# Attention of a four-layer transformer stack: heads in pairs, scores on two row tiles and values on two column tiles

## Chip, cores and metric

One core of one Trainium2 chip. The metric is the device time of one launch in microseconds (us); the median of several runs counts. "Engines" are TensorE (PE; PEld is its weight load), VectorE (DVE), ScalarE (ACT), GpSimd (POOL) and the DMA queues, of which SyncE (SP) issues the weights.

## What is computed

512 tokens of width 1024 go through two blocks of two layers each, all in float32. Attention stands in five places:

```python
# block 1, layer 0: 8 heads A (64 wide, three dilated windows, mixed by their log-sum-exp), 8 heads B (96 wide)
s = einsum(q, k) * scale;  o = softmax(s) @ v
# block 1, layer 1: 8 heads C, each the difference of two softmaxes
o = (softmax(s0) - lam * softmax(s1)) @ v          # v is 128 wide
# block 2, both layers: 4 heads each of
o_cmp = masked_softmax(q @ kc) @ vc                # 31 compressed keys
o_slc, o_win = causal softmax attention            # all blocks selected at 512 tokens
o = sigmoid(g0) * o_cmp + sigmoid(g1) * o_slc + sigmoid(g2) * o_win
o_fox = softmax(q @ k + c_q - c_k, causal) @ v     # with a decay
```

A's mixture of three windows equals one softmax in which key j counts as often as it lies in a window (`count`, 0 to 3). Around attention stand projections, feed-forward layers, norms and gates.

## The kernel before

Every activation is held transposed, features on the 128 partitions and the 512 tokens in the columns (`S` = 512, `P` = 128, `ST` = 4 tiles of tokens, `HD` = 64). Weights stream in 375 blocks of 512 KB through a ring of two. POOL splits each into a high and a low float32r part (L2131, L2134), the activations are split likewise by ACT and DVE, and TensorE makes three passes (`passes`, L681 to L683) into a PSUM bank. POOL can begin to split a block only when TensorE is done with the block two before it.

The program is written out by hand for each engine; engines meet by counting semaphores, and each engine's list is strictly in order. The stages are `mixer_a`, heads A, `mixer_b`, heads B, the output projection, norms and feed-forward, `mixer_c`, heads C, and so on; then, twice, `project_second`, `heads_second` and `merge`.

Attention (`attention`, one function for each engine) takes the heads one by one, and for each head its four tiles of 128 queries: such a step is a turn (`TURN_AT`). TensorE writes the scores of a turn into one of banks 0 to 3 (L742), three turns ahead of the rest (`AHEAD`), adds a mask or a decay by further matmuls (L745), and for the current turn transposes the exponentials `prob` (L775) into bank 4 or 5 and does one quarter of the values of the head before (L756). DVE takes the negated row maximum (L1648), ACT the exponentials (L1298) and the copy of the transposed ones into `pt` (L1285); for A, DVE makes that copy and multiplies it by `count` (L1639). The exponentials stay unnormalised: `v_ab`, `v_s`, `v_w` and `v_f` carry 64 columns of ones beside 64 of values, so that a 128-column values matmul gives the sum of each query's exponentials, 64 times over, in the other half of the bank. `divided` inverts those (two 32 x 32 transposes and a reciprocal, L1600 to L1603), multiplies by a gate where there is one, and by the values (L1683 to L1686); these steps are put behind later turns (`pending`, `FINISH_LAG`). The C heads differ: two scores for a turn, both banks exponentiated with row sums (`accum_out`), blended on DVE (`mixed`, L1626 to L1630) and then transposed; values there are 128 wide. The list `pending` also carries other DVE work in A (norms, splits and copies of `mixer_b`'s inputs) and in the second block (a convolution).

In `project_second` the three gates of each head are spread over 64 partitions each by six matmuls (`spread_gate`, L1031) into `gates`, and the compressed attention is done unnormalised as well: scores (L1046), exponentials, transposes (L1053), values and sums (`compressed_values`, L1060 and L1061), and division on DVE (L2023 to L2026).

In most runs of instructions a float32 matmul shows as two instructions in the trace.

## Time and profile before

| | us |
|---|---|
| median of 3 runs | 2795.81 |
| lowest and highest run | 2786.32, 2802.13 |
| span of the profiled execution | 2796.3 |
| TensorE busy | 2640.1 |
| DVE busy | 1359.9 |
| ACT busy | 657.1 |
| POOL busy | 1683.9 |

The profile is one execution. An engine's busy time is the union of its instructions; the chain of waits is followed back from the last instruction to what released each step. A time in a row is counted from the start of the span. Several instructions of the same kind in a row are merged into one line with their count, and the line's duration runs from the first start to the last end. A matmul's end is modelled: of two that follow closely, the second starts before the first ends, so the distance of starts says more than the durations. "Granted clock" is TensorE's, as a share of 2.4 GHz.

### The profile page before, as it was taken

Reading aid. Unit: us, or ns where it says so; the run is one execution under the profiler, and the core shown is the slowest. Engines: PE = TensorE matmul, PEld = TensorE weight load, DVE = VectorE, ACT = ScalarE, POOL = GpSimd, SP = SyncE. Lnnn points to the kernel's source line nnn. Section 1 sums busy time; section 2 is a strip of 40 time slices with the busy share of each in tenths; the row PEclk is TensorE's granted clock in tenths of the full one; section 3 lists DMA queues with packets and bytes.
Section 4 is the critical chain, followed back from the end, with each engine's and each line's share of the span. In section 5 each row is a group of like instructions: output and inputs, shape, how many; then the busy total and the mean of one; then the engine's idle time right before and its main releaser. Section 6 shows DMA issues by size and latency. Waiting matters only on the chain.

```text
span 2796.3 us, 30962 instructions
## 1 busy us (share of the span) xinstructions
PE 2640.1 (94%) x11138; PEld 1962.2 (70%) x11138; DVE 1359.9 (49%) x1615; ACT 657.1 (23%) x1110; POOL 1683.9 (60%) x756
## 2 busy tenths in 40 slices
PE   7998989999989978899999889999999899999998
PEld 6635568888867743678888677747888678478886
DVE  7476653220161888562211645565443545645343
ACT  2223423320021146132210231142010211421101
POOL 6603068887757720568887557605888676048785
PEclk9989999999999999999999999999999999999999
DMA  4201012222212210122222122201222222012222
GB/s 158 83 0 38 1 67 91 98 98 98 94 57 98 83 38 1 60 68 97 98 98 98 63 92 91 76 1 60 98 98 98 75 83 83 8 46 98 98 98 83
DMA packets 57543, 207.59 MB, mean 74 GB/s; under 512 B 6512, under 2 KB 6896, under 8 KB 57200
## 3 DMA queue, kind: packets, MB, share of 16 engines
q1 hardware_dynamic: 55872, 199.87, 21.2%
q10 hardware_dynamic: 1584, 6.49, 0.6%
q8 instruction: 64, 1.05, 0.2%
q14 instruction: 23, 0.19, 0.0%
HBM read 204.23 MB, written 2.10 MB: 74 GB/s over the span
## 4 chain that ended last, share of the span: by engine, by line
PE 84%; DVE 12%; POOL 1%; issue 1%; ACT 1%; DMA 0%; DVEq 0%; POOLq 0%; ACTq 0%
PE bank L681 23%; PE bank L683 22%; PE bank L682 22%; PE bank L742 5%; PE bank L756 4%; PE bank L775 2%; DVE region L1610 2%; PE bank L745 1%; DVE negmax L1648 1%; DVE x L1852 1%; PE bank L805 1%; DVE region L1589 1%; DVE prob L1630 1%; DVE moving_lo L1843 1%; DVE moving_lo L1595 1%
## 5 line engine op out<-in xcount | busy, mean ns | idle before, releaser
L2131 POOL TENSOR_TENSOR w_hi<-ring,unit 128x1024 fp32r<-128x1024 f32 x375 | 727.7, 1941 | 1063.2 <-PE bank L683 1058.1
L2134 POOL TENSOR_TENSOR w_lo<-ring,w_hi 128x1024 fp32r<-128x1024 f32 x375 | 955.6, 2548 | 29.5
L681 PE MATMUL bank<-moving_hi,w_hi 128*128 128x512 f32 x2138 | 853.0, 399 | 55.5 <-DVE moving_lo L1843 19.6
L682 PE MATMUL bank<-moving_lo,w_hi 128*128 128x512 f32 x2138 | 841.4, 394 | 0.0
L683 PE MATMUL bank<-moving_hi,w_lo 128*128 128x512 f32 x2138 | 841.2, 393 | 0.0
L681 PEld LDWEIGHTS bank<-moving_hi,w_hi 128*128 128x128 f32 x2138 | 406.5, 190 | 164.5 <-issue 44.8
L683 PEld LDWEIGHTS bank<-moving_hi,w_lo 128*128 128x128 f32 x2138 | 406.6, 190 | 87.2
L682 PEld LDWEIGHTS bank<-moving_lo,w_hi 128*128 128x128 f32 x2138 | 407.4, 191 | 85.4 <-issue 2.9
L742 PE MATMUL bank<-region 64*128 64x512 f32 (+2 forms) x448 | 198.9, 612 | 10.8 <-ACT region L1464 4.1
L1648 DVE TENSOR_REDUCE negmax<-bank 128x1 f32<-128x512 f32 (+1 forms) x224 | 131.8, 602 | 122.4 <-PE bank L745 84.7
L756 PE MATMUL bank<-region 128*128 128x512 f32 (+3 forms) x384 | 167.1, 525 | 1.7 <-ACT region L1285 0.9
L1298 ACT ACTIVATE prob<-bank,negmax 128x512 f32<-128x512 f32 (+1 forms) x224 | 137.1, 615 | 90.0 <-DVE negmax L1648 90.0
L2082 DVE TENSOR_TENSOR region<-region,bank 128x512 f32<-128x512 f32 x64 | 39.7, 683 | 243.3 <-PE bank L683 243.3
L1825 DVE SCALAR_TENSOR_TENSOR region<-x,bank 128x512 f32<-128x512 f32 x32 | 21.3, 686 | 274.1 <-PE bank L683 274.0
L742 PEld LDWEIGHTS bank<-region 64*128 64x128 f32 (+1 forms) x448 | 64.3, 199 | 110.8 <-issue 80.0
L681 PE MATMUL bank<-hid_hi,w_hi 128*128 (+1 forms) x352 | 137.8, 391 | 0.0
L683 PE MATMUL bank<-hid_hi,w_lo 128*128 (+1 forms) x352 | 137.0, 389 | 0.0
L682 PE MATMUL bank<-hid_lo,w_hi 128*128 (+1 forms) x352 | 136.9, 389 | 0.0
L1551 ACT ACTIVATE region<-bank 128x512 f32<-128x512 f32 x64 | 38.3, 598 | 373.8 <-PE bank L683 373.7
L775 PE MATMUL bank<-tabs,prob 128*128 128x128 f32 x624 | 107.6, 287 | 15.1 <-DVE prob L1630 14.7
L775 PEld LDWEIGHTS bank<-tabs,prob 128*128 128x128 f32 x624 | 74.9, 146 | 66.1 <-DVE prob L1630 41.6
L1865 DVE SCALAR_TENSOR_TENSOR region<-bank,cols,region 128x511 f32<-128x511 f32 x44 | 33.0, 749 | 181.5 <-ACT region L1399 181.5
(236 smaller groups left out, 3146.9 us busy)
## 6 DMA issues: line engine op xcount, KB each, us to landing
ring<-in_weights SPq DMA_DIRECT2D x375, 512.0 KB, 3.2
x<-in_x_t ACTq DMA_DIRECT2D x4, 512.0 KB, 8.4
out<-region SPq DMA_DIRECT2D x8, 256.0 KB, 2.2
region<-in_tables ACTq DMA_DIRECT2D x1, 1824.0 KB, 8.7
region<-in_tables ACTq DMA_DIRECT2D x1, 1024.0 KB, 5.5
region<-in_p_t ACTq DMA_DIRECT2D x2, 512.0 KB, 5.4
region<-in_tables SPq DMA_DIRECT2D x1, 320.0 KB, 10.1
small_w<-in_small_w ACTq DMA_DIRECT2D x1, 320.0 KB, 5.8
```

Source lines behind the costliest of these rows:

```text
L681: pe.matmul(bank, lhs[0], rhs[0], start=start, stop=False, skip_group_check=True)
L682: pe.matmul(bank, lhs[0], rhs[1], start=False, stop=False, skip_group_check=True)
L683: return pe.matmul(bank, lhs[1], rhs[0], start=False, stop=stop, skip_group_check=True)
L742: mm = pe.matmul(bank[:, 0:w], q(u, c)[:, i * P:i * P + P], k(u, c)[:, 0:w], start=True, stop=True)
L756: mm = pe.matmul(psum[6 + n % 2][:, lo:S], v(u, t), pt[:, n % 2, t, lo:S], start=(t == 0), stop=(t == ST - 1), skip_group_check=True)
L775: mm = pe.transpose(psum[4 + t % 2][:, kt * P:kt * P + P], prob[:, s % 4, kt * P:kt * P + P], ident)
L1298: act.activation(prob[:, s % 4, 0:w], psum[s % 4][:, 0:w], ACT.Exp, bias=negmax[:, s % 8:s % 8 + 1], accum_out=rowsum[:, s % 8:s % 8 + 1] ...
L1610: dve.scalar_tensor_tensor(out=dst, in0=src, scalar=gains(n), in1=rstd[:, buf, :], op0=ALU.mult, op1=ALU.mult).then_inc(normed, 1)
L1648: dve.tensor_reduce(negmax[:, s % 8:s % 8 + 1], psum[s % 4][:, 0:w], AX_X, ALU.max, negate=True).then_inc(maxed, 1)
L2082: ins = dve.tensor_tensor(t[:, i, :], t[:, i, :], psum[4 + i][:], ALU.mult)
L2131: pool.tensor_tensor(w_parts[0][:, s, :], ring[:, s, :], unit[:, 0:1].broadcast_to([P, BLK]), ALU.mult).then_inc(split_hi, 1)
L2134: pool.tensor_tensor(w_parts[1][:, s, :], ring[:, s, :], w_parts[0][:, s, :].bitcast(F32), ALU.subtract).then_inc(split_ready, 1)
```

## The change

- Two heads form a unit (slc, win and fox likewise; C keeps its two components). A turn does both heads; there are half as many turns. `AHEAD` is 2 instead of 3, the scores of two turns fill banks 0 to 3, and `prob` holds two turns.
- The scores of the pair follow each other, the first head on rows 0-63 and the second on rows 64-127 (for A and the second block; a B head has 96 rows, and its two follow each other on the whole array). The fox decay moves from 4 rows to 64 (zeros elsewhere), with a third row set, `decay_q1`.
- ACT takes row sums with each exponential (`accum_out`). DVE inverts them and multiplies `prob` by them, and by the gate in slc and win, ahead of the transposes (`normalised`). The ones beside the values, `divided`, `gates`, `spread_gate` and the memsets of ones go; a finished unit is one copy out of PSUM.
- Each value matmul is 64 columns wide, head c of the pair on column tile c of bank 6 or 7, over 256 queries (`pt_half`, half a unit at a time). Values of slc and win of a pair add up in the same bank, which two matmuls of the compressed attention (`vc_bd`, `cmp_pt`) open at the start of `heads_second`.
- Transposes of a turn go to banks 4 and 5, one for each head, so a turn's transposes wait for the copy of the turn before (`pt_stored`).
- A: the mask matmul goes and `count` becomes `log_count`, which DVE adds in a `tensor_tensor_reduce` that also gives the row extreme and writes its sum to `prob`; ACT exponentiates from there. DVE's write has to wait for the transposes of two turns before.
- The copies of the transposed probabilities are all ACT's, two banks by one instruction; in B and the second block, and in C, one reduction covers two banks.
- The compressed softmax is normalised on DVE before its transposes (four instructions), and the gate logits are transposed (`gate_columns`, four transposes and one ACT copy).

The removed lines of the functions that are rewritten as a whole stand in the listing above and are left out here.

```diff
-    units = [("A", h) for h in range(A_HEADS)] + [("B", h) for h in range(B_HEADS)]
+    units = [("A", j) for j in range(A_HEADS // 2)] + [("B", j) for j in range(B_HEADS // 2)]
     units += [("C", h) for h in range(C_HEADS)]
     for layer in range(DEPTH):
-        units += [("slc", layer, h) for h in range(4)] + [("win", layer, h) for h in range(4)]
-        units += [("fox", layer, h) for h in range(4)]
+        units += [(kind, layer, j) for j in range(2) for kind in ("slc", "win")]
+        units += [("fox", layer, j) for j in range(2)]
     return units
+def group_of(u):
+    return ("nsa",) + u[1:] if u[0] in ("slc", "win") else u
 UNITS = attention_units()
-SCORES = [(u, q, c) for u in UNITS for q in range(ST) for c in range(2 if u[0] == "C" else 1)]
-SCORE_AT = {key: n for n, key in enumerate(SCORES)}
-TURNS = [(u, q) for u in UNITS for q in range(ST)]
+TURNS = [(u, i) for u in UNITS for i in range(ST)]
 TURN_AT = {key: n for n, key in enumerate(TURNS)}
-UNIT_AT = {u: n for n, u in enumerate(UNITS)}
+GROUPS = list(dict.fromkeys(group_of(u) for u in UNITS))
+GROUP_AT = {u: GROUPS.index(group_of(u)) for u in UNITS}
...
+            def scores(u, i, q, k, extra, causal=False):
+                t = TURN_AT[(u, i)]
+                if t >= 2:
+                    pe.wait_ge(exped, 2 * t - 2)
+                w = (i + 1) * P if causal else S
+                at = [banks[:, 2 * (t % 2) + c, 0:w] for c in range(2)]
+                for c in range(2):
+                    mm = pe.matmul(at[c], q(u, c)[:, i * P:i * P + P], k(u, c)[:, 0:w], start=True, stop=True)
+                for more in extra(u):
+                    for c in range(2):
+                        o, lhs, rhs = more(at[c], u, c, i)
+                        mm = pe.matmul(o, lhs, rhs, start=False, stop=True, skip_group_check=True)
+                mm.then_inc(scored, 1)
+            def heads_in_pairs(units, q, k, v, extra, causal=False, seeded=False):
                 turns = [(u, i) for u in units for i in range(ST)]
...
+                halves = [(u, h) for u in units for h in range(2)]
+                def values(u, h, tiles):
+                    g = GROUP_AT[u]
+                    opens = not seeded or u[0] == "fox"
+                    last = 2 * h + 1 if causal else ST - 1
+                    for t in tiles:
+                        if t == 0:
+                            pe.wait_ge(pt_stored, TURN_AT[(u, 2 * h + 1)] + 1)
+                            if h == 0 and opens and g >= 2:
+                                pe.wait_ge(attended, g - 1)
+                        lo = max(t * P - 2 * P * h, 0) if causal else 0
+                        for c in range(2):
+                            mm = pe.matmul(psum[6 + g % 2][HD * c:HD * c + HD, 2 * P * h + lo:2 * P * h + 2 * P], v(u, t, c),
+                                           pt_half[:, h, c, t, lo:2 * P], start=(opens and h == 0 and t == 0),
+                                           stop=(t == last), skip_group_check=True)
+                    if h == 1 and tiles[-1] == last and u[0] != "slc":
+                        mm.then_inc(weighed, 1)
+                def tiles_of(h, part):
+                    n = h + 1 if causal else 2
+                    return range(part * n, part * n + n)
+                for u, i in turns[:AHEAD]:
+                    scores(u, i, q, k, extra, causal)
+                for n, (u, i) in enumerate(turns):
+                    if n + AHEAD < len(turns):
+                        scores(*turns[n + AHEAD], q, k, extra, causal)
+                    t = TURN_AT[(u, i)]
+                    if t >= 1:
+                        pe.wait_ge(pt_stored, t)
+                    for c in range(2):
+                        pe.wait_ge(scaled, 2 * t + c + 1)
+                        for kt in range(i + 1 if causal else ST):
+                            mm = pe.transpose(psum[4 + c][:, kt * P:kt * P + P],
+                                              prob[:, 2 * (t % 2) + c, kt * P:kt * P + P], ident)
+                    mm.then_inc(turned, 1)
+                    if n >= 2:
+                        u, h = halves[n // 2 - 1]
+                        values(u, h, tiles_of(h, n % 2))
+                u, h = halves[-1]
+                values(u, h, [*tiles_of(h, 0), *tiles_of(h, 1)])
...
+                heads_in_pairs([u for u in UNITS if u[0] == kind], q, k, v, lambda u: [])
...
+            def gate_columns(layer):
+                pe.wait_ge(stored, T["stored"][("gsig", layer)])
+                for i in range(ST):
+                    mm = pe.transpose(psum[6][:, i * P:i * P + P], gate_sig[:, i * P:i * P + P], ident)
+                mm.then_inc(spread, 1)
...
-            def compressed_values(layer):
-                pe.wait_ge(prepared, T["prepared"][("cmp_pt", layer)])
-                for j in range(2):
-                    pe.matmul(psum[4 + j][:], vc_bd[:, j, :], prob[:, 3, :], start=True, stop=True)
-                    mm = pe.matmul(psum[6 + j][:], ones_bd[:, j, :], prob[:, 3, :], start=True, stop=True)
+                    mm = pe.transpose(psum[7][:, i * P:i * P + P], cmp_p[:, i * P:i * P + P], ident)
...
+                pe.wait_ge(prepared, T["prepared"][("cmp_pt", layer)])
+                g = GROUP_AT[("slc", layer, 0)]
+                pe.wait_ge(attended, g)
+                for j in range(2):
+                    pe.matmul(psum[6 + (g + j) % 2], vc_bd[:, j, :], cmp_pt, start=True, stop=True, skip_group_check=True)
...
+                def decay(bank, u, c, i):
+                    return bank, (decay_q0, decay_q1)[u[2]][half(c), i * P:i * P + P], decay_k[half(c), 0:i * P + P]
+                def diagonal(bank, u, c, i):
+                    return bank[:, i * P:i * P + P], ident_bf[:], tri_bf[:]
+                extra = lambda u: [decay, diagonal] if u[0] == "fox" else [diagonal]
+                heads_in_pairs([u for u in UNITS if len(u) == 3 and u[1] == layer], q, k, v, extra, causal=True, seeded=True)
...
+            def attention(units, blend=False, causal=False, masked=False):
                 turns = [(u, i) for u in units for i in range(ST)]
...
                 def copy_turned(u, i):
...
+                    t, g = TURN_AT[(u, i)], GROUP_AT[u]
                     act.wait_ge(turned, t + 1)
...
+                    if blend:
+                        if i == 0:
+                            act.wait_ge(weighed, g - 1)
+                        act.activation(pt[:, g % 2, :, i * P:i * P + P],
+                                       psum[4 + t % 2].rearrange("p (k q) -> p k q", k=ST), ACT.Copy).then_inc(pt_stored, 1)
+                        return
+                    kt, lo = i + 1 if causal else ST, i % 2 * P
+                    act.activation(pt_half[:, i // 2, :, 0:kt, lo:lo + P],
+                                   banks[:, 4:6, 0:kt * P].rearrange("p c (k q) -> p c k q", k=kt),
                                    ACT.Copy).then_inc(pt_stored, 1)
                 for n, (u, i) in enumerate(turns):
...
+                    t = TURN_AT[(u, i)]
+                    w = (i + 1) * P if causal else S
+                    for c in range(2):
+                        act.wait_ge(maxed, 2 * t + c + 1)
+                        if c == 0 and t >= 2:
+                            act.wait_ge(turned, t - 1)
+                        p, at = prob[:, 2 * (t % 2) + c, 0:w], 2 * (t % 4) + c
+                        act.activation(p, p if masked else psum[2 * (t % 2) + c][:, 0:w], ACT.Exp, bias=negmax[:, at:at + 1],
+                                       scale=-1.0 if masked else 1.0, accum_out=rowsum[:, at:at + 1]).then_inc(exped, 1)
+                    if n:
                         copy_turned(*turns[n - 1])
...
+            def attention(units, evacuate, blend=False, causal=False, masked=False, gate=None, first=()):
                 turns = [(u, i) for u in units for i in range(ST)]
...
+                def normalised(u, i):
+                    t = TURN_AT[(u, i)]
+                    at = 2 * (t % 4)
+                    w = (i + 1) * P if causal else S
+                    dve.wait_ge(exped, 2 * t + 2)
+                    link(dve.reciprocal(rownorm[:, at:at + 2], rowsum[:, at:at + 2]))
+                    for c in range(2):
+                        p, by = prob[:, 2 * (t % 2) + c, 0:w], rownorm[:, at + c:at + c + 1]
+                        g = gate(u, c, i) if gate else None
+                        dve.tensor_scalar(p, p, by, g, ALU.mult, ALU.bypass if g is None else ALU.mult).then_inc(scaled, 1)
+                def finish(u):
+                    g = GROUP_AT[u]
+                    dve.wait_ge(weighed, g + 1)
+                    dve.tensor_copy(evacuate(u), psum[6 + g % 2]).then_inc(attended, 1)
+                pending = [step if type(step) is tuple else (0, step) for step in first]
                 for n, (u, i) in enumerate(turns):
...
+                    t = TURN_AT[(u, i)]
+                    w = (i + 1) * P if causal else S
+                    b, at = 2 * (t % 2), 2 * (t % 4)
+                    dve.wait_ge(scored, t + 1)
+                    if masked:
+                        if t >= 2:
+                            dve.wait_ge(turned, t - 1)
+                        for c in range(2):
+                            dve.tensor_tensor_reduce(
+                                out=prob[:, b + c, :], in0=psum[b + c], in1=log_count[:, i, :], scale=-1.0, scalar=3.0e38,
+                                op0=ALU.add, op1=ALU.min, accum_out=negmax[:, at + c:at + c + 1]).then_inc(maxed, 1)
+                    else:
+                        dve.tensor_reduce(negmax[:, at:at + 2], banks[:, b:b + 2, 0:w], AX_X, ALU.max,
+                                          negate=True).then_inc(maxed, 2)
+                    if n:
+                        (blended if blend else normalised)(*turns[n - 1])
+                    before = units[max(n // ST - 1 - blend, 0)]
+                    if i == 3 - 2 * blend and n > ST * (1 + blend) and before[0] != "slc":
+                        finish(before)
+                    elif pending and pending[0][0] <= n:
                         pending.pop(0)[1]()
...
+                (blended if blend else normalised)(*turns[-1])
+                for u in units[-1 - blend:]:
+                    finish(u)
...
+                stored_at("cmp_exp")
+                total, share = cmp_negmax[:, :], cmp_negmax.rearrange("p (i h) -> p i h", i=ST)
+                rows = rstd[:, 1, :].rearrange("p (a n) -> p a n", n=CMP_N)
+                link(dve.tensor_reduce(total, rows, AX_X, ALU.add))
+                link(dve.reciprocal(total, total))
+                link(dve.tensor_tensor(share, share, gate_col[:, :, 0:4], ALU.mult))
+                dve.tensor_tensor(cmp_p.rearrange("p (a n) -> p a n", n=CMP_N), rows,
+                                  total.unsqueeze(2).broadcast_to([P, 16, CMP_N]), ALU.mult).then_inc(prepared, 1)
+                dve.wait_ge(compress_step, 4 * layer + 4)
+                dve.tensor_tensor(cmp_pt, psum[7][:], tab("cmp_mask", S), ALU.mult).then_inc(prepared, 1)
...
-                for j in range(2):
-                    inv = rope_tmp[:, j, :]
-                    link(dve.tensor_scalar(inv, psum[6 + j][:], 0.5, None, ALU.max))
-                    inverse(std[:, j, :], inv, slice(0, P))
-                    link(dve.tensor_tensor(inv, std[:, j, :], gates[:, 0, j, :], ALU.mult))
-                    dve.tensor_tensor(mix[:, j, :], psum[4 + j][:], inv, ALU.mult).then_inc(prepared, 1)
```

## Rows read from the trace of the kernel before

**Rows 1.** The page's part 1: busy time, share of the span, instructions.

```profile
PE 2640.1 (94%) x11138; PEld 1962.2 (70%) x11138; DVE 1359.9 (49%) x1615; ACT 657.1 (23%) x1110; POOL 1683.9 (60%) x756
```

**Rows 2.** The page's part 4: the chain that ended last, by engine.

```profile
PE 84%; DVE 12%; POOL 1%; issue 1%; ACT 1%; DMA 0%; DVEq 0%; POOLq 0%; ACTq 0%
```

**Rows 3.** Stages: stretch, its us, busy us and count by engine, clock, DMA.

```profile
135.00:234.00 99.00, 98.12 (x287) 38.97 (x288) 72.84 (x117) 21.98 (x32) 0.00 (x0) 0.86 0.00 1
272.00:342.00 70.00, 69.60 (x257) 36.69 (x257) 45.29 (x74) 37.57 (x64) 2.15 (x1) 1.00 0.02 8
1006.00:1106.00 100.00, 84.62 (x319) 33.33 (x320) 90.42 (x200) 65.05 (x166) 0.00 (x0) 0.97 0.00 1
1658.00:1808.00 150.00, 142.14 (x722) 115.94 (x720) 81.33 (x72) 29.70 (x48) 107.67 (x48) 0.97 0.24 81
1808.00:1902.60 94.60, 94.06 (x377) 46.33 (x377) 64.10 (x116) 42.69 (x98) 0.57 (x1) 0.93 0.02 6
```

**Rows 4.** TensorE by time, A heads: start, us, engine, line, tile, shapes, count.

```profile
188.56 1.12 PE L742 MATMUL bank<-region 64*128 64x512 f32 x2
189.61 0.39 PE L745 MATMUL bank<-region,ident_bf 128*128 128x512 bf16 x1
189.84 0.60 PE L775 MATMUL bank<-tabs,prob 128*128 128x128 f32 x4
190.28 1.02 PE L756 MATMUL bank<-region 128*128 128x512 f32 x2
191.23 1.12 PE L742 MATMUL bank<-region 64*128 64x512 f32 x2
```

**Rows 5.** Order of time, TensorE, B heads: scores of one turn and the next.

```profile
291.61 1.02 PE L742 MATMUL bank<-region 96*128 96x512 f32 x2
...
293.77 1.02 PE L742 MATMUL bank<-region 96*128 96x512 f32 x2
```

**Rows 6.** Order of time, TensorE, C heads; in brackets idle before and its releaser.

```profile
1042.56 1.13 PE L742 MATMUL bank<-region 64*128 64x512 f32 x4
1044.48 0.66 PE L775 MATMUL bank<-tabs,prob 128*128 128x128 f32 x4 [0.79 <-DVE prob L1630]
```

**Rows 7.** Order of time, second block, layer 0; PEld is the weight load.

```profile
1803.57 0.19 PEld L683 LDWEIGHTS bank<-moving_hi,w_lo 128*128 128x128 f32 x1
...
1804.11 1.93 PE L1135 MATMUL bank<-region,small_w 64*64 64x512 f32 x8
```

**Rows 8.** Lines of VectorE, 135 to 234 us; busy, mean ns, idle before.

```profile
L1639 DVE TENSOR_TENSOR region<-bank,region 128x512 f32<-128x512 f32 x32 | 21.8, 685 | 1.0 <-PE bank L775 0.7
```

**Rows 9.** Lines with shapes apart, whole span; last, one instruction by time.

```profile
L1648 DVE TENSOR_REDUCE negmax<-bank 128x1 f32<-128x512 f32 x152 | 101.5, 687 | 92.1 <-PE bank L745 55.5 <-PE bank L742 35.8
...
L1629 DVE TENSOR_SCALAR prob<-prob,rownorm 128x512 f32<-128x512 f32 x32 | 15.6, 486 | 1.1
...
L1648 DVE TENSOR_REDUCE negmax<-bank 128x1 f32<-128x128 f32 x24 | 7.0, 291 | 12.8 <-PE bank L745 12.2
...
1736.72 1.22 DVE L1971 TENSOR_TENSOR_SCAN region<-region 128x512 f32<-128x512 f32 x1
```

**Rows 10.** Stretches of 4 us in A and C: busy and granted clock.

```profile
160.00:164.00 4.00, 4.00 (x11) 1.29 (x9) 1.78 (x3) 0.28 (x1) 0.00 (x0) 0.70 0.00 0
...
1014.00:1018.00 4.00, 2.80 (x13) 0.97 (x12) 3.82 (x10) 3.10 (x9) 0.00 (x0) 1.00 0.00 0
```

**Rows 11.** Second-block projections: a group, then VectorE in order of time.

```profile
L1031 PE MATMUL bank<-region 128*128 128x512 f32 x24 | 12.5, 602 | 0.0
...
1756.51 0.69 DVE L1992 TENSOR_TENSOR prob<-bank,region 128x512 f32<-128x512 f32 x1 [9.76 <-PE bank L1053]
```

**Rows 12.** Order of time, TensorE, second-block heads.

```profile
1845.56 0.70 PE L742 MATMUL bank<-region 64*128 64x256 f32 x2
1846.19 0.23 PE L745 MATMUL bank<-tri_bf,ident_bf 128*128 128x128 bf16 x1
1846.26 0.50 PE L775 MATMUL bank<-tabs,prob 128*128 128x128 f32 x3
```

364 lines of the change are left out of this document (105 added, 259 removed).

## The prediction

> **What bounds the kernel now.** I read the page's engine list first, then its chain of waits, then the busy time stage by stage, then single turns. TensorE is busy for 2640 of 2796.3 us [rows 1], and the chain that ends last is 84% TensorE [rows 2]. So an edit pays where it takes work off TensorE's queue, and costs where TensorE begins to wait. Most of the chain is the three-pass weight blocks (L681 to L683), which the change leaves alone. By stage [rows 3]: the A heads take 99.0 us, the B heads 70, the C heads 100, and the heads of the second block 94.6 us in each layer (layer 1 reads 94.4). TensorE is over 98% busy in A, B and the second block, with VectorE at 73 of 99 us in A. C is the other way round: VectorE is busy 90 of 100 us, and TensorE's own transposes wait for it by 0.79 us in a turn [rows 6].
>
> A turn of one A head is scores, mask, four transposes, values, and takes 2.67 us from scores to scores (188.56 to 191.23) [rows 4]. By the start times the parts are worth 1.05, 0.23, 0.44 and 0.95 us. In B the same turn without a mask takes 2.16 us (291.61 to 293.77) [rows 5], where A's without its mask would take 2.44. B's scores use 96 rows of the array and need the same tiling as their neighbours; A's use 64. The 0.28 us is what going to 64-row tiles and back costs, 0.14 us for one change; a plain 512-column matmul is worth 0.86.
>
> **What the paired scores are worth.** C shows it already: four score instructions (two heads' worth, on rows 0-63 and 64-127) take 1.13 us [rows 6] where A's two take 1.12 [rows 4]. They run side by side. So a pair's scores cost 1.05 us instead of 2.10 in A and the second block. B's 96 rows cannot be paired: 2 x 0.86 stays.
>
> **What the values on two column tiles are worth.** No instruction before has 128 rows and 64 columns. The nearest is L1135: four matmuls (eight instructions) of 64 rows by 64 columns, on opposite corners of the array, in 1.93 us [rows 7]. One after the other they would need 4 x 0.86 = 3.44; so different columns run side by side when the rows differ too. Here both tiles take the same 128 rows. From below, then, half the time: a turn's values (two key tiles, two heads, 256 columns) 0.86 us; from above, no gain, 1.72 us. I take 0.86, the side L1135 is on.
> The Trainium skill (TensorE: Matmul & The Clock Gate, Part 3) speaks against it: a weight load overlaps a running matmul only when the row group differs, and these two tiles share theirs. The trace shows more overlap than that rule allows: a 128-row load of 0.19 us starts together with a 128-row matmul of 0.39 and lies under it [rows 7]. By the rule the values would come out near the serial case, 1.72 us a turn, which is the first rival below.
>
> **A heads** (16 pair turns instead of 32). TensorE: scores 0.86, transposes 8 x 0.107 = 0.87, values 0.86, three changes of tiling 0.42: 3.0 us. The mask matmul goes. VectorE: two masked reductions, two normalisations and a reciprocal. The masked reduction (adds log_count, writes the sum, keeps the extreme) is not in the trace; L1639 also joins a bank and a table at 0.685 us [rows 8], the scan L1971 carries a running result at 1.22 us [rows 9]. I take 0.685; the other end adds 32 x 0.535 = 17 us. Normalising is L1629 at 0.486 twice [rows 9], and C's reciprocal takes 0.155. Sum 2 x 0.685 + 0.155 + 2 x 0.486 = 2.50 us. VectorE now also waits for the transposes of the turn that it has just normalised, since it writes the masked scores into `prob` (two turns deep): 0.44 for the second head's transposes and 0.2 of hand-over, which nothing on VectorE's queue covers except a pending step. So the ring normalise, transpose, reduce sets the turn: 3.15 us, plus one evacuation (0.685) in four turns: 3.3 x 16 = 53 us. The pending latent steps stay: two normalisations of 3.8 and 3.1, five splits of 1.1, four spreads of 0.69, together 15.2; eleven waits of 0.6 cover 6.6 of it, 8.6 remains. Start 1.3, drain (transposes 0.87, copy 1.1, values 1.72) 3.7. The inverses and count multiplications on VectorE go, and ScalarE gets the copies. In C it does two exponentials and a one-bank copy in each of 32 turns, 65.05 / 32 = 2.0 us [rows 3]; a second bank adds 0.6 at most, and 2.6 lies beside VectorE's 3.3, hidden. 53 + 8.6 + 1.3 + 3.7 = 66.6.
> The clock: before, A runs its first 28 us at the lower level, 1.2 GHz, after a stall of TensorE, and rises to 2.4 GHz between 160 and 164 us, 3 us after its first values instruction [rows 10]. In C, with scores on both row halves, it is up by 1014, some 7 us after the first scores and before any values. I expect C's course: 4 us lost. A = 71, against 99: **-28**.
>
> **B heads.** TensorE: 1.72 + 0.87 + 0.86 + two changes of tiling 0.28 = 3.73, against 4.32 for two turns. 16 x 3.73 = 59.7, start and drain 3.3: 63 against 70: **-7**. VectorE's 2.5 and an evacuation fit under it.
>
> **C heads.** Same work; one reduction over two banks. L1648's 0.291 for 128 columns and 0.687 for 512 rise by 0.132 per 128 [rows 9], so 1024 cost 1.22 instead of 2 x 0.64: 32 x 0.06: **-2** (between -3 and +2, since the first exponential now waits for both maxima).
>
> **Second block, projections.** Six `spread_gate` and four `compressed_values` matmuls of 0.86 us go (L1031, two instructions of 0.602 that overlap) [rows 11]; four transposes (0.43) come. The last four lie among projections where TensorE never waits: -3.4. Spreads 0 and 1: -1.7. The others fill time in which TensorE would wait for POOL to split the next weights, which it can begin only when a block is done; they give 0.5. VectorE gets a third `decay` row and the compressed softmax, six instructions of 0.2 to 0.75 us (up to 2.7 beside POOL), ahead of TensorE's compressed transposes; before, VectorE has been idle for 9.76 us when those come [rows 11], so they are covered, at worst by a little. Per layer -5.2: **-10.5**.
>
> **Second block, heads.** For a pair of heads (four turns, 1+2+3+4 key tiles): scores 10 x 0.213 + 0.8 of tiling = 2.9; diagonals 8 x 0.07 = 0.6; transposes 20 x 0.107 = 2.2; values side by side 10 x 0.213 + 4 x 0.1 = 2.5; 8.2 us. The small parts are read from start to start: a diagonal to the transposes behind it 0.07, scores of 256 columns to their diagonal 0.63, 0.2 above 2 x 0.213 [rows 12]. Six pairs 49.3, decay matmuls in pairs 2.7: 52. VectorE for a pair: reductions 3.3, normalisations 3.6, evacuation 0.7: 7.6, nearly as much. With two engines this close and two turns in flight the waits do not all hide; C, where one engine leads, loses 0.8 us of TensorE a turn. I add a third of a microsecond a turn, 8 us, between 0 and 16. Start and drain 4, slow clock 3, the two seeding matmuls on `vc_bd` 1.7: 68.6 against 94.6: -26, twice **-52**.
>
> Sum: -28 - 7 - 2 - 10.5 - 52 = -99.5, and 2796.3 - 99.5 = 2696.8. That is against the profiled span; the median of the three runs, 2795.8, is 0.5 us below it, so I forecast **2696 us**.
>
> **Rivals.**
> *The column tiles run one after the other* (the change doesn't do what it says). A turn of A becomes 3.0 + 0.86 = 3.9 on TensorE against 3.3 to 3.9 on VectorE: +9. B: +13. Second block: 10 x 0.213 x 6 = 12.8 more on TensorE less the waits it fills, +10 each. 2696 + 42 = 2738.
> *The clock stays at 1.2 GHz through the A and second-block heads*, because TensorE waits more and transposes more. At that level A's turn is near twice its TensorE part, 6 us, so 95 us, and the second block's 94: 2696 + 24 + 2 x 25.5 = 2771. The rows speak against: in C between 1014 and 1018 TensorE is busy 2.8 of 4 us, a paired score and four transposes to each turn with no values, at the full clock [rows 10]. The Trainium skill (TensorE: Matmul & The Clock Gate, Part 4) says that transposes don't count as a busy TensorE in the same way, which would favour this rival; C's rows don't bear it out.
> *Every change from one column tile to the other drains the array*, as a change of row tiling does (0.14 to 0.2 us). There are 64 + 64 + 144 = 272 value matmuls after, which alternate between the tiles. My sum prices each at 0.21 us; serial is 0.43, and with a drain 0.6. The gain of 100 us is gone when each costs 0.37 more than forecast, 0.58. At 0.63 the time is 2696 + 272 x 0.42 = 2810: slower. For it: the tiling change is real. Against it: C alternates row tiles without one.
>
> **Chances.** Forecast 0.67, own range 2671 (waits in the second block hidden, no slow clock) to 2721 (masked reduction at its upper end, half the extra waits). Serial tiles 0.17; clock 0.05; drain 0.05; something else that takes most of the gain 0.06. The range 2670 to 2745 takes in the first two. Runs before lie within 0.6% of one another, so 0.5% (14 us) is about what can be told from no change. Faster 0.89, within 0.5% 0.05, slower 0.06.
>
> **What would show it.** A value pair (four instructions of 128*64) in about half the time of two full ones. A's stage near 71 us with TensorE waiting for `prob` by VectorE and VectorE for transposes. B near 63, TensorE-bound. Second-block heads near 69, projections 5 us shorter each, C unchanged. The masked reduction near 0.69. The prediction is wrong if value instructions of two tiles follow one another, if the masked reduction is well over 0.69 in a stage that VectorE bounds, or if the clock stays low after the first paired scores.

## The result, and the profile after

The changed kernel takes 2697.0 us (median of 4 runs, 2693.7 to 2704.3) against 2794.3 (4 runs beside it, 2786.3 to 2802.1): a ratio of 0.9656, 95% interval 0.963 to 0.968. The forecast was 2696. The profiled execution is the slowest of the four, with a span of 2702.5 us. Its page, parts 1 and 4 [rows 1, 2], and then its stages [rows 3], the columns as there:

```profile
PE 2514.6 (93%) x11306; PEld 1924.1 (71%) x11306; DVE 1281.2 (47%) x1564; ACT 671.8 (25%) x1212; POOL 1689.4 (63%) x755
...
PE 81%; DVE 15%; issue 1%; ACT 1%; POOL 1%; DMA 0%; DVEq 0%; ACTq 0%; POOLq 0%
```

```profile
137.00:201.00 64.00, 56.15 (x322) 29.05 (x323) 52.38 (x141) 39.20 (x80) 0.00 (x0) 0.87 0.00 1
238.00:301.00 63.00, 60.94 (x321) 33.28 (x321) 42.67 (x80) 38.25 (x80) 1.82 (x1) 1.00 0.03 9
964.00:1065.00 101.00, 84.78 (x320) 32.94 (x319) 88.29 (x167) 66.36 (x167) 0.00 (x0) 0.97 0.00 1
1608.00:1770.00 162.00, 150.09 (x728) 123.57 (x727) 83.76 (x76) 31.00 (x49) 110.74 (x48) 0.90 0.22 75
1770.00:1836.00 66.00, 59.19 (x428) 33.08 (x428) 46.33 (x107) 43.76 (x122) 0.58 (x1) 0.97 0.03 9
2155.00:2313.00 158.00, 145.79 (x729) 120.31 (x729) 83.60 (x76) 31.02 (x49) 111.05 (x48) 0.94 0.22 77
2313.00:2379.00 66.00, 59.28 (x429) 32.96 (x429) 46.32 (x107) 43.73 (x121) 0.39 (x1) 0.97 0.03 9
```

From the first matmul of one stage to that of the next, in us:

| stretch | before | after | change | forecast |
|---|---|---|---|---|
| start to A's first scores | 135.1 | 137.0 | +1.9 | 0 |
| A heads | 99.0 | 63.6 | -35.4 | -28 |
| B heads | 69.7 | 63.1 | -6.6 | -7 |
| C heads | 100.0 | 101.6 | +1.6 | -2 |
| projections, layers 0 and 1 | 158.4, 157.2 | 162.3, 158.3 | +3.9, +1.1 | -5.2, -5.2 |
| second-block heads, each layer | 94.5 | 66.1 | -28.4 | -26 |
| all the rest | 1887.9 | 1884.4 | -3.5 | 0 |

So the total came out well by luck, because two errors met: the heads of A and of the second block gained 12 us more than forecast (7.4 and twice 2.4), and the projections, from which 10.4 was due, became 5.0 us longer.

One turn of an A pair, in order of time (TensorE and VectorE; compare [rows 4]); the last line is a later turn:

```profile
175.74 1.08 PE L758 MATMUL bank<-region 128*64 128x256 f32 x8
175.95 0.69 DVE L1662 CUSTOM_DVE_ANT_0 prob<-bank,region 128x512 f32<-128x512 f32 x1 [0.24 <-PE bank L779]
...
176.75 1.13 PE L734 MATMUL bank<-region 64*128 64x512 f32 x4
...
177.38 0.88 DVE L1645 TENSOR_SCALAR prob<-prob,rownorm 128x512 f32<-128x512 f32 x2
...
178.01 1.06 PE L779 MATMUL bank<-tabs,prob 128*128 128x128 f32 x8
...
179.00 1.08 PE L758 MATMUL bank<-region 128*64 128x256 f32 x8
...
179.22 0.69 DVE L1662 CUSTOM_DVE_ANT_0 prob<-bank,region 128x512 f32<-128x512 f32 x1 [0.24 <-PE bank L779]
...
189.02 0.69 DVE L1662 CUSTOM_DVE_ANT_0 prob<-bank,region 128x512 f32<-128x512 f32 x1 [0.96 <-PE bank L779]
```

A turn is 3.27 us (175.95 to 179.22). L1662 is the masked reduction, 0.69 us, and each reduction waits for the transposes L779: 0.24 us behind a turn in which VectorE also did a pending step of 0.69, and 0.96 behind one in which it did not.

### The profile page after: what moved, and what is told of

Read it like the earlier page. It is cut to its first block, busy times and chain, and to the rows that moved or that the text cites. A ratio compares the mean times of both kernels' runs of the same rounds, so it can differ in the third digit from the quotient of the medians.

```text
span 2702.5 us, 31180 instructions
## 1 busy us (share of the span) xinstructions
PE 2514.6 (93%) x11306; PEld 1924.1 (71%) x11306; DVE 1281.2 (47%) x1564; ACT 671.8 (25%) x1212; POOL 1689.4 (63%) x755
## 3 DMA queue, kind: packets, MB, share of 16 engines
q8 instruction: 65, 1.06, 0.2%
## 4 chain that ended last, share of the span: by engine, by line
PE 81%; DVE 15%; issue 1%; ACT 1%; POOL 1%; DMA 0%; DVEq 0%; ACTq 0%; POOLq 0%
PE bank L678 24%; PE bank L680 23%; PE bank L679 23%; PE bank L734 3%; DVE negmax L1666 2%; PE bank L779 2%; PE bank L758 2%; DVE region L1613 2%; DVE region L1592 1%; PE bank L842 1%; DVE moving_lo L1598 1%; DVE x L1839 1%; POOL w_lo L2105 1%; DVE moving_lo L1830 1%; DVE prob L1632 1%
## 5 line engine op out<-in xcount | busy, mean ns | idle before, releaser
L734 PE MATMUL bank<-region 64*128 64x512 f32 (+3 forms) x448 | 131.5, 604 | 11.1 <-DVE region L1592 4.4
L680 PE MATMUL bank<-hid_hi,w_lo 128*128 (+1 forms) x352 | 137.0, 389 | 0.0
L679 PE MATMUL bank<-hid_lo,w_hi 128*128 (+1 forms) x352 | 137.0, 389 | 0.0
L1666 DVE TENSOR_REDUCE negmax<-bank 128x2 f32<-128x1024 f32 (+2 forms) x96 | 98.1, 1022 | 65.3 <-PE bank L738 35.0
L1312 ACT ACTIVATE prob<-bank,negmax 128x512 f32<-128x512 f32 (+2 forms) x192 | 114.6, 604 | 40.1 <-DVE negmax L1666 39.8
L1390 ACT ACTIVATE region<-region 128x512 f32<-128x512 f32 x32 | 19.2, 630 | 342.5 <-DVE region L1823 342.5
L1592 DVE TENSOR_TENSOR region<-region,rope_tmp 128x512 f32<-128x512 f32 (+3 forms) x43 | 98.4, 2288 | 1.4
L678 PE MATMUL bank<-w_hi,moving_hi 128*128 128x512 f32 (+2 forms) x232 | 80.2, 346 | 17.6 <-DVE moving_lo L1598 17.6
L734 PEld LDWEIGHTS bank<-region 64*128 64x128 f32 (+1 forms) x448 | 42.0, 195 | 69.7 <-issue 57.2
```

Source lines behind the costliest of these rows:

```text
L678: pe.matmul(bank, lhs[0], rhs[0], start=start, stop=False, skip_group_check=True)
L679: pe.matmul(bank, lhs[0], rhs[1], start=False, stop=False, skip_group_check=True)
L680: return pe.matmul(bank, lhs[1], rhs[0], start=False, stop=stop, skip_group_check=True)
L734: mm = pe.matmul(at[c], q(u, c)[:, i * P:i * P + P], k(u, c)[:, 0:w], start=True, stop=True)
L1312: act.activation(p, p if masked else psum[2 * (t % 2) + c][:, 0:w], ACT.Exp, bias=negmax[:, at:at + 1], scale=-1.0 if masked else 1.0, acc ...
L1592: ins = dve.tensor_tensor(out, tile[at], tmp[at], ALU.add)
```

## Experiments

### Why the projections gained nothing

Between 40 and 80 us into layer 0's projections the changed kernel shows this: stretches of 10 us (columns as above, the clock third from the end), then TensorE's waits in them, in brackets:

```profile
1648.00:1658.00 10.00, 9.33 (x38) 7.38 (x39) 7.26 (x6) 0.60 (x1) 7.42 (x4) 0.83 0.29 105
1658.00:1668.00 10.00, 7.72 (x25) 6.12 (x25) 3.35 (x2) 0.00 (x0) 7.42 (x4) 0.66 0.26 97
1668.00:1678.00 10.00, 7.63 (x34) 6.06 (x33) 4.40 (x3) 0.60 (x1) 8.30 (x4) 0.78 0.18 62
1678.00:1688.00 10.00, 7.10 (x34) 6.01 (x33) 0.45 (x2) 2.49 (x4) 5.82 (x4) 0.84 0.16 52
```

```profile
1648.67 0.50 PE L678 MATMUL bank<-moving_hi,w_hi 128*128 128x512 f32 x1 [1.43 <-POOL w_lo L2105]
1660.89 0.79 PE L678 MATMUL bank<-moving_hi,w_hi 128*128 128x512 f32 x1 [2.27 <-POOL w_lo L2105]
1674.33 0.77 PE L678 MATMUL bank<-moving_hi,w_hi 128*128 128x512 f32 x1 [2.37 <-POOL w_lo L2105]
1687.51 0.76 PE L678 MATMUL bank<-moving_hi,w_hi 128*128 128x512 f32 x1 [2.90 <-POOL w_lo L2105]
```

TensorE waits for POOL's split, and behind the three longer waits of this layer the block begins at 1.2 GHz (its first matmul takes 0.76 to 0.79 us, not 0.50). Theory K: the removed spread_gate matmuls had stood in these waits; without them the granted clock falls, and that eats what they cost. Rivals: POOL's splits set the pace of the stage (P), VectorE's and ScalarE's new steps set it (V), or the clock falls by chance, whatever TensorE does (C).

**e1_fill**, nine matmuls put back into the changed kernel at the places of the removed ones:

```diff
+            def fill(layer, n=1):
+                pe.wait_ge(stored, T["stored"][("gcol", layer)])
+                for _ in range(n):
+                    pe.matmul(psum[6][:], ident, gate_sig, start=True, stop=True)
...
```

> The changed kernel with TensorE work put back into each layer's projections where the changed kernel dropped it: five matmuls of 512 columns at the places of spread_gate 1 to 5 and four at that of compressed_values, all into a bank that nobody reads; nothing is left out. By their prices in the kernel before (0.86 us, of which 3 to 5 of the nine lie in waits for POOL) they cost about 5 us a layer. Theory K (the projections gained nothing because the removed matmuls had filled TensorE's waits for weights, and without them the granted clock falls to 1.2 GHz and the work behind runs slowly): the clock stays near 1.0 between the first projection and the heads, the stage goes from 162.4 back to 158 to 160 us in each layer, and the kernel is 3 to 9 us faster than the changed one (2688 to 2694). Rival P (the stage is held by POOL's weight splits, the clock is a consequence): the fillers vanish in the waits, 162 to 163, no change in all. Rival V (the added VectorE and ScalarE steps of the new softmax hold it): the four late fillers add 3.4 a layer, 166, the kernel 5 to 8 us slower.

Measured: 2695.3 us (2689.7 to 2701.0); the median does not tell it from the changed kernel. K's 2688 to 2694 is missed by 1 us. Projections 155.0 and 157.9 us at a mean clock of 0.98 and 0.95: shorter than the 158 to 160 of K, though TensorE has more to do than in the changed kernel. For K, thinly.

**e2_thin**, the kernel before with only the removed matmuls made short:

```diff
-                pe.matmul(psum[6][:], sel[:, n // 2, n % 2, :], gate_sig, start=True, stop=True).then_inc(spread, 1)
+                pe.matmul(psum[6][:, 0:HD], sel[:, n // 2, n % 2, :], gate_sig[:, 0:HD], start=True, stop=True).then_inc(spread, 1)
```

(and the four of compressed_values alike)

> The kernel before with only its spread_gate and compressed_values matmuls cut from 512 to 64 columns (so the gates reach 64 of 512 tokens: that part of the computation is left out); VectorE, ScalarE and POOL keep all their work. Theory K: the projections don't gain the 5 us a layer that the shorter matmuls are worth; the granted clock drops to 1.2 GHz in 1650 to 1720 where it was 1.00, the stage is 158.4 to 163 us, the whole between 2793 and 2803. Rival V (the matmuls were worth 5 us, the changed kernel's other edits ate it): clock as before, the stage 153 to 154, the whole 2784 to 2787. Rival P: the stage 155 to 157 (only the four late ones pay), clock lower without a price, the whole 2788 to 2791.

Measured: 2801.3 us (2792.5 to 2803.7, 10 runs) beside 2794.8; ratio 1.0009 (0.9991 to 1.0028). The interval begins at 2792.3 us, so V's 2784 to 2787 and P's 2788 to 2791 are both outside. Projections 157.1 and 161.0 at 0.94 and 0.92. Ten matmuls a layer cut to an eighth bought nothing, with VectorE, ScalarE and POOL untouched: that is my forecast of -5.2 falling, shown in the kernel before.

**e8_fill_more**, the changed kernel with the five early fillers of e1_fill and five more in the waits that were left:

```diff
                 compress(layer, 1)
+                fill(layer)
...
                 compress(layer, 2)
+                fill(layer)
...
                 compress(layer, 3)
+                fill(layer, 3)
```

> The changed kernel with the five early fillers of the first filler run, without its four late ones, and five more where TensorE there still waited for POOL's split: one behind compress 1, one behind compress 2, three behind compress 3 (waits of 1.10, 1.19 and 2.90 us). Nothing is left out. Theory K (the granted clock falls behind TensorE's waits in the projections and that eats what the removed matmuls saved): the clock stays at 1.00 from the first filler on, the projections take 150 to 155 us in both layers (162.3 and 158.3 in the changed kernel, 155.0 and 157.9 with the first fillers) and vary less. Rival P (POOL's splits set the pace): no shorter than 155. Rival C (the clock falls whatever TensorE does, by chance): windows under 1.00 as before, 155 to 162 at random.

Measured: 2686.6 us (2686.1 to 2688.6), ratio 0.9608 (0.958 to 0.9636). Projections 152.4 and 154.0. The same stretch as above, and its waits:

```profile
1646.00:1656.00 10.00, 10.00 (x50) 7.59 (x49) 8.34 (x7) 0.60 (x1) 8.57 (x5) 1.00 0.34 105
1656.00:1666.00 10.00, 9.83 (x46) 7.10 (x46) 5.29 (x4) 0.60 (x1) 9.03 (x5) 1.00 0.34 107
1666.00:1676.00 10.00, 9.75 (x52) 7.73 (x52) 5.17 (x4) 1.88 (x2) 8.94 (x5) 1.00 0.32 105
1676.00:1686.00 10.00, 9.14 (x37) 6.37 (x37) 1.40 (x6) 1.39 (x4) 8.24 (x4) 1.00 0.32 105
```

```profile
1657.72 0.50 PE L678 MATMUL bank<-moving_hi,w_hi 128*128 128x512 f32 x1 [0.17 <-POOL w_lo L2119]
1668.05 0.47 PE L678 MATMUL bank<-moving_hi,w_hi 128*128 128x512 f32 x1 [0.25 <-POOL w_lo L2119]
1678.38 0.48 PE L678 MATMUL bank<-moving_hi,w_hi 128*128 128x512 f32 x1 [0.25 <-POOL w_lo L2119]
```

Ten more matmuls that nobody reads, and the stage is about 6 us shorter. P falls (152.4 is under its 155). POOL gets ahead too: its share of these stretches rises from 5.8 to 8.3 us in ten to 8.2 to 9.0, because a block done sooner frees its buffer sooner.

**e13_changed**, the changed kernel once more:

> The changed kernel itself once more, beside the others on one chip. Theory K: again windows at 1.2 GHz between 40 and 110 us of each layer's projections, 155 to 163 us long, their length going with the sum of the clock's deficit; whole 2692 to 2700. Rival: the projections come out at 152 to 154 by themselves.

Measured: 2698.5 us (2696.7 to 2700.6, 5 runs); projections 159.0 and 161.0 at a clock of 0.92. Against C stand all profiles together. Eight of them (the changed kernel's two and those of the six experiments below that leave its projections alone) give 16 such stretches: 155.1 to 162.4 us, mean 159.8, with clocks of 0.96 down to 0.90 in nearly the same order. With ten fillers, four stretches: 152.4 to 154.1, mean 153.6, clocks 0.96 to 0.97. How often the clock falls differs from one execution to the next, hence the spread of 7 us, and nothing here shows what decides it: in the changed kernel's first profile it is low around layer 0's wait of 2.27 us (0.66 in the row above) and stays at 1.00 from 2203 to 2213 us, around layer 1's wait of 2.28. But that it falls there at all goes with the waits.

**e12_before_fill**, five fillers in the kernel before, which keeps its spreads:

```diff
                 compress(layer, 1)
+                fill(layer, "g4")
...
                 compress(layer, 2)
+                fill(layer, "g5")
...
                 compress(layer, 3)
+                fill(layer, "g5", 3)
```

> The kernel before, which still has its spread matmuls, with five fillers a layer more in TensorE's waits for POOL (one behind compress 1, one behind compress 2, three behind compress 3). Nothing is left out. Theory K: there the clock dips only at these waits, so the projections go from 158.4 and 157.2 to 154 to 157 and the whole is 2 to 8 us faster than 2795. Rival P or C: nothing, or 2 us slower for the matmuls added.

Measured: 2793.4 us beside 2795.4, ratio 0.9985 (0.9967 to 1.0003): not told from nothing. Projections 155.6 and 155.7 against 158.4 and 157.2, one profile of each: in K's range, but too few to count.

### What bounds A

**e4_own_buffer**, masked scores in buffers of their own, so that the reduction waits for ScalarE's read of them and not for the transposes:

```diff
+        masked_s = [place(120, 2, S), place(124, 2, S)]
...
-                            dve.wait_ge(turned, t - 1)
+                            dve.wait_ge(exped, 2 * t - 2)
...
-                                out=prob[:, b + c, :], in0=psum[b + c], in1=log_count[:, i, :], scale=-1.0, scalar=3.0e38,
+                                out=masked_s[t % 2][:, c, :], in0=psum[b + c], in1=log_count[:, i, :], scale=-1.0, scalar=3.0e38,
```

(and ScalarE's exponential reads from `masked_s`)

> The changed kernel with the masked scores of A written into buffers of their own instead of into prob, so VectorE's reduction no longer waits for the transposes; nothing is left out. Theory R (my forecast's: A's turn of 3.27 us is the ring normalise, transpose, reduce): the turn falls to TensorE's own work, by my forecast 3.0 us, A from 63.6 to 59 to 60, the whole 3 to 5 us faster. Rival T (TensorE's own turn is 3.27: 1.13 + 0.99 + 1.02 and the changes of tiling, and the ring only happens to be as long): A stays at 63.6 within 0.7 us, VectorE's waits move from the transposes to the scores, the whole within 1 us.

Measured: 2697.3 us (2696.4 to 2698.6). A takes 60.7 us, and its turn 3.10 (175.75 to 178.85 by the scores). The same 32 us of A, first in this kernel, then in the changed one:

```profile
161.00:193.00 32.00, 31.76 (x212) 17.39 (x212) 29.34 (x83) 25.12 (x53) 0.00 (x0) 1.00 0.00 1
```

```profile
161.00:193.00 32.00, 30.67 (x200) 16.11 (x196) 27.84 (x78) 23.58 (x50) 0.00 (x0) 1.00 0.00 1
```

So the ring did set the turn, by 0.17 us; under it lies TensorE's own turn of 3.10 (3.0 forecast), at which it is 99% busy. Two later kernels with the same edit show A at 61.1 and 60.3, against 63.6 to 65.1 in five profiles without. Three us of 2697 are less than the medians can tell.

**e9_warm_a**, that kernel with eight matmuls on constants in TensorE's waits at the start of A (three ahead of the first scores, two ahead of the third, three ahead of the first transposes):

```diff
+            def warm(n, bank=5):
+                for _ in range(n):
+                    pe.matmul(psum[bank], ident, tabs[:, 0:S], start=True, stop=True)
...
```

> The own-buffer kernel with eight matmuls of 512 columns into a free bank at the start of A, where TensorE waits: three ahead of A's first scores (a wait of 2.3 us for the rotation), two ahead of the third scores and three ahead of the first transposes (2.6 us). Nothing is left out. Theory K: the clock is at 1.00 from A's first scores instead of from 155, so A goes from 60.7 to 56 to 58 us. Rival V (in those first turns VectorE, 92% busy with the latent steps, sets the pace and the slow clock lies under it): the clock rises, A stays at 60 to 61.5.

Measured: 2694.0 us (2693.5 to 2697.1); A 61.1 us. The first 8 us of A, here and in e4_own_buffer:

```profile
131.00:139.00 8.00, 7.48 (x23) 2.50 (x20) 6.90 (x17) 2.83 (x7) 0.00 (x0) 1.00 0.00 0
```

```profile
137.00:145.00 8.00, 5.31 (x12) 1.54 (x12) 6.10 (x13) 2.00 (x5) 0.00 (x0) 0.55 0.01 2
```

The clock went from 0.55 to 1.00 there, and over all of A from 0.86 to 0.94, and A was no shorter: V. At A's start VectorE has the latent steps before it (the pending norms and splits of `mixer_b`'s inputs), and a fast TensorE only waits longer. K is a rule for stretches that TensorE bounds.

### Row tiles and column tiles, priced

**e3_one_column**, both heads' values on one column tile:

```diff
-                            mm = pe.matmul(psum[6 + g % 2][HD * c:HD * c + HD, 2 * P * h + lo:2 * P * h + 2 * P], v(u, t, c),
+                            mm = pe.matmul(psum[6 + g % 2][0:HD, 2 * P * h + lo:2 * P * h + 2 * P], v(u, t, c),
```

> The changed kernel with the values of both heads of a pair put on the same 64 columns of the array: same instructions, same count and columns, one column tile. (The second head's values add to the first's rows, so the mixed outputs of A, B and the second block are not computed rightly and half of them are missing.) Theory S (two column tiles of the same 128 rows run side by side): a turn's eight value instructions go from 1.08 to about 1.9 us; A's turn 3.27 to 4.1 (stage 63.6 to 76), B's 3.80 to 4.65 (63.1 to 77), the heads of the second block 66.1 to 76 to 79 in each layer; the whole 2696 + 13 + 14 + 22 = 2740 to 2750. Rival (they were not side by side; a 64-column tile is only cheaper because its weight load is short): nothing changes, within 3 us.

Measured: 2745.0 us (2737.8 to 2747.5). A 72.9, B 76.1, second-block heads 76.5 in each layer: +9.3, +13.0, +10.4. In order of time, the values of a turn and its neighbours:

```profile
180.00 1.94 PE L758 MATMUL bank<-region 128*64 128x256 f32 x8
181.87 1.13 PE L734 MATMUL bank<-region 64*128 64x512 f32 x4
```

1.94 us for the eight instructions that take 1.08 on two tiles. The tiles run side by side.

**e6_one_row**, the scores of both heads from rows 0 to 63:

```diff
-                    return qk_a[half(c), u[1], :] if u[0] == "A" else q_b[0:B_QK, 2 * u[1] + c, :]
+                    return qk_a[half(0), u[1], :] if u[0] == "A" else q_b[0:B_QK, 2 * u[1] + c, :]
```

(and so for the keys, the second block and its decay rows)

> The changed kernel with the scores of both heads of a pair of A and of the second block (and their decay rows) read from rows 0 to 63: same instructions, one row tile, so the second head's scores are those of the first (its own are left out). It prices the row tiles alone. Theory (scores of two row tiles run side by side, 1.13 us a pair, and one after the other 1.7 to 2.0): A's turn 3.27 to 4.1, A 63.6 to 77; B unchanged at 63.1; the second block's heads 66.1 to 78 to 82 in each layer; whole 2735 to 2745. Rival (the gain came from the column tiles and fewer changes of tiling, row tiles add little): A under 68, second block under 70.

Measured: 2741.4 us (2734.7 to 2743.3). A 75.9, B 63.1, second-block heads 78.7: +12.3, 0, +12.6. Its scores:

```profile
181.71 1.98 PE L734 MATMUL bank<-region 64*128 64x512 f32 x4
```

1.98 against 1.13. Undone, the row tiles cost 37.5 us in all and the column tiles 43.1 (the sums over A, B and both layers).

**e7_column_order**, both key tiles of one column tile, then both of the other:

```diff
-                    for t in tiles:
...
-                        for c in range(2):
+                    for c in range(2):
+                        for t in tiles:
```

> The changed kernel with the value matmuls of a turn in another order: both key tiles of the first column tile, then both of the second, instead of in turns. Nothing is left out. Theory S (two column tiles run side by side only when they stand next to each other in TensorE's queue): of four matmuls only the middle two overlap, half of what one column tile cost: A 63.6 to 68, B 63.1 to 70, the second block's heads 66.1 to 71, whole 2708 to 2722. Rival D (a change of column tile costs something, as one of row tiling does): fewer changes, so faster than 2696. Rival Q (the array takes them side by side whatever their order): within 2 us of 2696.

Measured: 2703.7 us (2702.2 to 2704.7), 5 above e13_changed beside it, and so in none of the three ranges. The row of the values decides. The values of a turn:

```profile
179.62 1.09 PE L758 MATMUL bank<-region 128*64 128x256 f32 x8
```

1.09 us: unchanged. In the trace the second tile's first matmul starts 0.013 us behind the first tile's, although the first tile's other matmuls stand between them in the queue. So my theory that only neighbours in the queue overlap falls (A 65.1, not 68), and so does the idea that a change of column tile costs something: Q is left. The second-block heads are 67.1 instead of 66.1 in each layer; why, no row that I read shows. The projections, which this edit does not touch, took 162.1 and 160.7 here.

### C

**e5_c_two**, two reductions of one bank:

```diff
+                    elif blend:
+                        for c in range(2):
+                            dve.tensor_reduce(negmax[:, at + c:at + c + 1], psum[b + c], AX_X, ALU.max, negate=True).then_inc(maxed, 1)
```

> The changed kernel with C's maximum taken by two reductions of one bank each, as before the change; nothing is left out. C took 100.0 us before and 101.6 after. Theory (the joint reduction wins 0.07 us a turn, loses it again between the scale and the blend that follow it, and the extra 1.6 us lies at the start and end, since the first exponential waits for both maxima): with two reductions the start wins back 0.7, the turn is 2.77 to 2.85, C 100 to 103, of which the first three turns take 4.5 instead of 4.8. Rival (the joint reduction costs time in each turn): turn under 2.77 and C under 100.

Measured (one run): a turn of 2.84 us against 2.78, and from C's first scores to the next weight block 119.3 us against 118.1 (116.5 before). By the measure of the table above C takes 102.7 us, in the range forecast. The joint reduction is a gain of 0.06 a turn, as forecast, so its time in the turn is not what made C longer. Its lines and the blend's, VectorE, with the idle time before them; first after, then before:

```profile
L1666 DVE TENSOR_REDUCE negmax<-bank 128x2 f32<-128x1024 f32 x32 | 39.0, 1219 | 3.6 <-PE bank L734 3.6
L1632 DVE SCALAR_TENSOR_TENSOR prob<-prob,rownorm 128x512 f32<-128x512 f32 x32 | 24.1, 752 | 3.3
```

```profile
L1648 DVE TENSOR_REDUCE negmax<-bank 128x1 f32<-128x512 f32 x64 | 41.0, 682 | 2.6 <-PE bank L742 2.6
L1630 DVE SCALAR_TENSOR_TENSOR prob<-prob,rownorm 128x512 f32<-128x512 f32 x32 | 24.0, 751 | 1.1
```

The engine now stands idle for 3.3 us ahead of the blends of 32 turns where it was 1.1: as much as the reduction saved (41.0 to 39.0). The joint reduction is not the reason, for e5_c_two, with two reductions, shows the same 3.3; the operands and the wait ahead of the blend are those of before, and the reason stays open. The 1.6 us lie elsewhere, for the most part at the start. The fourth turn's reduction starts 10.37 us behind C's first scores, where it was 9.37; in e5_c_two it is 9.99, so 0.4 of that 1.0 goes with the joint reduction. The other 0.6 both have, and there the reduction waits for scores:

```profile
973.92 1.23 DVE L1666 TENSOR_REDUCE negmax<-bank 128x2 f32<-128x1024 f32 x1 [0.51 <-PE bank L734]
```

In the kernel before it does not wait there. Scores now come two turns ahead instead of three (`AHEAD`), which would explain it; no run tests that.

### The better version

**e11_both**, e4_own_buffer's edit and e8_fill_more's:

> The changed kernel with both edits that paid: A's masked scores in buffers of their own and the ten fillers in each layer's projections. Nothing is left out. Theory K and theory R add up: A 60.7, projections 152 to 155 in both layers, whole 2682 to 2688. Rival (the 10 us of the filled kernel were the luck of one loading): 2690 to 2697.

Measured: 2687.3 us (2683.6 to 2691.2, 5 runs), ratio 0.9617 (0.9594 to 0.964), beside e13_changed at 2698.5 (2696.7 to 2700.6) on the same chip: no run of one reaches the other's. A 60.3, projections 154.0 and 154.1. e8_fill_more alone does as well (2686.6). Both beat the changed kernel by about 11 us.

## Why the prediction was right, and where it was not

- *Paired scores.* 1.05 us for two heads from start to start. In e4_own_buffer, where TensorE does not wait, it is 1.06 (175.75 to the transposes at 176.81); by length the four instructions take 1.13, and 1.98 one after the other (e6_one_row). Right.
- *Values on two column tiles.* 0.86 forecast from L1135 [rows 7]; 1.02 from start to start (179.00 to the next scores at 180.02), the change of tiling within it. Right in kind, shown by e3_one_column. The Trainium skill (TensorE: Matmul & The Clock Gate, Part 3) has weight loads overlap running matmuls only where the row group differs. Here two tiles of the same 128 rows take 1.08 us for what takes 1.94 on one, and in the turn at 179.00 the next weight load of these rows starts 0.05 us behind the start of the first matmul, which runs for 0.43; so the measurement decides against it. The first rival was priced at +9, +13 and +10 and cost +9.3, +13.0 and +10.4: the rows before were enough to price it. The third rival falls with e7_column_order.
- *A heads.* The masked reduction was taken at 0.685 and is 0.69; the ring was forecast as what binds, at 3.15 a turn and 3.3 with its share of the evacuation, and is 3.27, with the evacuation under the wait (e4_own_buffer shows the ring). 16 turns are 52.3. TensorE's own turn was put at 3.0 and is 3.10. The terms that failed are those around it: latent steps 8.6, start 1.3, drain 3.7, slow clock 4, together 17.6, where 11.3 was measured. I let waits of 0.6 us cover the pending steps; the waits are 0.96, so a step of 0.69 costs nothing at all. And the slow clock lay under VectorE's work, so the 4 us for it were not there to pay: in e9_warm_a it is 1.00 at the start of A, and A is no shorter.
- *B heads.* 3.73 a turn forecast, 3.80 measured:

```profile
252.51 1.98 PE L734 MATMUL bank<-region 96*128 96x512 f32 x4
254.33 1.04 PE L779 MATMUL bank<-tabs,prob 128*128 128x128 f32 x8
255.30 1.08 PE L758 MATMUL bank<-region 128*64 128x256 f32 x8
256.31 1.98 PE L734 MATMUL bank<-region 96*128 96x512 f32 x4
```

- *C heads.* -2 forecast, +1.6 measured, within what I had allowed (+2). My reason for it, the first exponential that waits for both maxima, is good for 0.4 by e5_c_two; the rest is not shown.
- *Projections.* The step that failed: "The others fill time in which TensorE would wait for POOL to split the next weights, which it can begin only when a block is done; they give 0.5", and the -3.4 and -1.7 beside it. I priced the removed matmuls as work, at a clock held fixed, and did not ask what they did for the clock. With the clock kept up the stage does come out at 152.4 to 154.1, where 153.2 and 152.0 were forecast. The Trainium skill (TensorE: Matmul & The Clock Gate, "Why this matters for your kernels") warns of pauses between bursts of matmuls, after which the array runs at half its rate. The trace shows it in part: 0.66 around a wait of 2.27 us in layer 0, but 1.00 around one of 2.28 in layer 1. I had used that page for the rival in the heads and not here.
- *Second-block heads.* 68.6 forecast, 66.1 measured. TensorE's own work, with the slow clock, was 56.7 and is 59.2; waits, start and drain were 12 and are 6.9. Two errors again, the larger in the waits: a third of a microsecond a turn on top of a start and a drain was too much.
- *Clock rival.* The clock is 0.87 in A, where that costs nothing, and 0.97 in the second block's heads. It did bite, in the stage where I had not looked for it.
- *Sum.* Against the span: 2696.8 forecast, 2702.5 measured in that execution, 2692 to 2699 in the other eight of this kernel. What made the kernel faster was forecast with its mechanism, within 12 us; that the median came within 1 us of the forecast is luck.

## What to carry to other kernels

Before you take matmuls out of a stage that waits for its weights, look whether they stand in the waits: there they cost nothing and help to hold the clock, and without them blocks behind the waits can run at 1.2 GHz; ten idle matmuls, 8.6 us of work by their price, made the stage 6 us shorter. That holds only where TensorE is the bound. A step that an engine does while it waits in a ring is free up to the length of that wait, so read the wait in the turn without the step before charging it. And where the total comes out right, compare stage by stage: here errors of +15 and -12 us had met.

## What the runs showed of the hardware

- Two column tiles of the same 128 rows work side by side whatever their order in the queue: eight fp32 instructions of 256 columns in 1.08 us in turns, 1.09 in groups (the second tile's start 0.013 us behind the first's), 1.94 on one tile.
- The reduction that adds a table, writes the sum and keeps the row's extreme costs what a plain two-operand instruction of 512 columns does (0.69 us; the next starts 0.61 to 0.62 behind it), with the 0.08 us read of its accumulator under the next one.
- The stretch ahead of A's first scores takes 130.5 to 137.1 us in kernels that are equal up to there (the changed kernel, e3_one_column and e4_own_buffer among them). In the changed kernel's first profile (137.0) the clock is 0.56 between 40 and 50 us; in the second (130.9) it stays at 1.00. That difference of 6 us is more than half of the spread between the runs of one kernel (10.7 us).
- With POOL's waits filled the clock still dips, to 0.66 to 0.86 over 10 us, about 90 us into the projections (e8_fill_more, e11_both), where TensorE counts as fully busy, behind the 32-column matmuls of the compressed scores. What would hold it there was not tried.
